# Boundaries between the blocks of a decoder step on one core: awaited stores, early loads, a later start of compression

## The chip, the cores and the metric

One core of a Trainium2 chip runs the whole step, one launch. The metric is the time of one launch in microseconds, the median of the runs shown.

## The reference

One layer of a decoder for two groups: a prompt of 1024 tokens, and 8 sample sequences with 4 new tokens each behind 8192 cached ones (all float32, model width 1024, heads of 64).

```
h = RMSNorm(x);  q, k, v, gates = h @ w_in
mixer A (8 heads): dilated windows (128,1), (512,4), (2048,16), merged by their denominators
mixer B (8 query heads, 2 key heads): compressed blocks of 64 tokens (an MLP over each),
  the 16 best blocks per token (gathered), and a window of 512; merged by sigmoid gates
every logit gets a bias from a table of relative positions
x += concat[A | B] @ w_out
h = RMSNorm(x);  u = h @ w_up;  causal depthwise convolution of width 3 (with kept state for samples)
x += (SiLU(gate) * value) @ w_down;  y = RMSNorm(x)
```
The caches, moved on by the new rows, are outputs too.

## The kernel before

The program is five blocks, each in a function of its own and run one after the other by `hybrid_step` (L3030). A block ends for each engine with its last instruction, a DRAIN, and a barrier of all engines (the lines of these are those on which a block is opened: L294, L1179, L1815, L865, L2372); then its semaphores are cleared (`Mem.end`, L65 to L69), with another barrier.

`front` (L150) projects all 1056 rows and compresses the sample caches. Its PE works through a list of jobs written out at L170 to L193: bias tables (b), transposes of x (x), projections by column chunk and row tile (n, s, f), transposes of keys (k), and queries and keys by chunk and group of rows (q). Compression is worked in 17 items of two halves. A half is one entry ("comp") in the order, 64 matmuls at L539 for the first item, over cache rows that POOL gathers and DVE turns (L721 for the first item, L730 for the others). L214 to L237 put the comps between the jobs: from job `first_c` on, one at most behind each job, spaced by the columns that the jobs multiply, and done 28000 columns ahead of the end. POOL issues the stores of results (L807 to L818) from five buffers and, last, waits for all of them and for the compressed rows of the prompt (L820 to L822).

`compressed_and_dilated` (cd, L1165) does the compressed branch for both groups and the dilated branch of the samples. SP issues its constants and queries (`qs`, `qp`, L1347 to L1359), then items of the dilated branch, the stores of the prompt's compressed output (L1373), the window keys for the block behind (L1377), and stores the dilated output to `mixT` in DRAM (L1382), which it waits for (L1384).

`sample_selected` (sb, L1804) does the selected and the window branch of the samples. SP loads the choice (L1942), the new keys (`knew`, L1944, L1945), window values, new values (L1947 to L1950), and at the end stores to `mixT` (L1953) and waits (L1955). ACT issues the window's bias `BW` in eight pieces (L2219) ahead of its copies. POOL gathers the chosen pages by indirect DMA (L116, L1974) and adds up their bias (L1984). PE starts with transposes of the new keys (L2011) and the window keys (L2017), later does the cached keys (L2080). DVE takes the window's scores with `BW` (L2259 to L2266).

`prompt_attention` (pa, L834) goes over 12 pairs of heads (3 kinds of 4), each in 8 query tiles. For a pair SP loads queries, keys, values and the bias of two heads (L920 to L936) into one of two buffers; POOL reverses the queries (L1036); PE multiplies (L969), transposes (L992) and multiplies by the values (L1012). At pair 9 SP loads `mixT` and, on 20 partitions, the state and weights of the convolution (`cv`, L953 to L955).

`ffn` (L2355) begins with the samples' part of the output projection (L2593), transposes `cv` (L2704), and then goes over all row tiles (L2611) and the up and down projections (L2652, L2730, L2680). Its SP starts with the rows of x (L2529) and an identity (L2530).

## Time and profile before

| | us |
|---|---|
| median of 3 runs | 2256.63 (2254.52 to 2258.96) |
| profiled execution | 2255.5 |
| its span, first to last instruction | 2253.5 |
| PE busy | 2108.8 (94%) |
| DVE / ACT / POOL busy | 1014.1 / 519.7 / 474.6 |
| mean granted clock of PE | 0.968 |

The span in 40 slices of 56 us, busy tenths of PE, its clock, and the DMA share:

```profile
PE   6989999997967885999999999999999999999998
...
PEclk9999999998788997999999999999999999999999
DMA  7467477643577996122251313665666332500200
```

A digit is the busy share of a slice in tenths. Front ends in the tenth slice, cd in the twelfth, sb in the sixteenth, pa in the twenty-second; the rest is ffn. "PEq", "SPq" are the sequencers of an engine: waits, branches and DMA issues.

### The profile page before, as it was taken

To read this page: it belongs to the slowest core of one execution; us is meant where nothing else is said; L and a number is where in the kernel's file an instruction comes from. 1 tells how busy PE (TensorE), PEld (TensorE's weight loads), DVE (VectorE), ACT (ScalarE), POOL (GpSimd) and SP (SyncE) were. 2 spreads that over 40 slices of the span, in tenths; PEclk is the share of its full clock that TensorE was granted. 3 is DMA by queue.
4 is the path that set the end of the run, shared out by engine and by line. 5 is a ranking of instruction groups with operands and counts; after the bars stand their busy time and mean duration, and the time that the engine had idled before them with its cause. 6 is when DMAs were issued, how large, how long until landed. Compare 5 with 4: busy or idle time off the path is not lost. (4 is left out here: it accounts for less than half of the span.)

```text
span 2253.5 us, 31733 instructions
## 1 busy us (share of the span) xinstructions
PE 2108.8 (94%) x12498; PEld 1374.5 (61%) x12498; DVE 1014.1 (45%) x2435; ACT 519.7 (23%) x1101; POOL 474.6 (21%) x667
## 2 busy tenths in 40 slices
PE   6989999997967885999999999999999999999998
PEld 3445466664635664666676446888888888544443
DVE  4044455402425543666676225667776765200110
ACT  3111101012213432776676111111111111000100
POOL 1434234102014650112222001223232222000000
PEclk9999999998788997999999999999999999999999
DMA  7467477643577996122251313665666332500200
GB/s 212 160 214 281 186 283 291 238 152 93 206 282 286 385 397 224 58 90 85 78 157 40 118 66 132 224 204 187 224 223 207 132 98 90 188 1 10 78 21 19
DMA packets 150649, 372.78 MB, mean 165 GB/s; under 512 B 36871, under 2 KB 89087, under 8 KB 132448
## 3 DMA queue, kind: packets, MB, share of 16 engines
q1 hardware_dynamic: 120678, 149.37, 21.0%
q0 software_dynamic: 25280, 149.44, 17.0%
q10 hardware_dynamic: 4544, 71.95, 9.0%
q8 instruction: 100, 1.64, 0.3%
q14 instruction: 47, 0.38, 0.1%
HBM read 343.42 MB, written 98.60 MB: 196 GB/s over the span
## 5 line engine op out<-in xcount | busy, mean ns | idle before, releaser
L2652 PE MATMUL ff_ps<-ff_hx,ff_aw 128*128 128x264 f32 x2464 | 550.1, 386 | 0.9 <-DVE ff_hx L2891 0.9
L2652 PEld LDWEIGHTS ff_ps<-ff_hx,ff_aw 128*128 128x128 f32 x2464 | 467.3, 190 | 80.8 <-issue 1.2
L730 DVE STREAM_TRANSPOSE sel_space<-sel_space 128x512 f32<-128x512 f32 x256 | 155.4, 674 | 165.6 <-PE in_psH L539 165.6
L503 PE MATMUL in_ps<-in_w,in_xT 128*128 128x512 f32 (+1 forms) x512 | 201.5, 547 | 0.0
L1113 DVE CUSTOM_DVE_ANT_0 pa_L<-pa_psS,pa_T 128x512 f32<-128x512 f32 (+3 forms) x288 | 138.9, 532 | 59.4 <-PE pa_psS L969 58.3
L1093 ACT ACTIVATE pa_L<-pa_L,pa_nm 128x640 f32<-128x640 f32 (+3 forms) x192 | 141.9, 741 | 45.1 <-DVE pa_nm L1123 43.2
L503 PEld LDWEIGHTS in_ps<-in_w,in_xT 128*128 128x128 f32 x512 | 95.0, 191 | 93.5 <-issue 87.6
L539 PE MATMUL in_psH<-sel_space 128*64 128x256 f32 (+1 forms) x1152 | 123.1, 369 | 11.2 <-DVE sel_space L721 11.2
L969 PE MATMUL pa_psS<-pa_kT,pa_qT 64*128 64x512 f32 (+3 forms) x576 | 114.9, 505 | 18.6 <-POOL pa_qT L1036 18.6
L628 ACT ACTIVATE in_yout<-in_ps 128x128 f32<-128x128 f32 (+5 forms) x88 | 41.3, 480 | 390.4 <-PE in_ps L503 213.4
L3013 DVE TENSOR_TENSOR ff_work<-ff_ps,ff_work 128x512 f32<-128x512 f32 (+1 forms) x18 | 12.3, 685 | 238.0 <-PE ff_ps L2730 139.3
L517 PE MATMUL in_ps<-in_xT,in_w 128*128 128x352 f32 x384 | 116.9, 462 | 0.0
L539 PEld LDWEIGHTS in_psH<-sel_space 128*64 128x64 f32 x1152 | 76.5, 142 | 59.6 <-issue 25.6
L992 PE MATMUL pa_psT<-pa_ident,pa_L 128*128 128x128 f32 x816 | 112.0, 281 | 0.4 <-DVE pa_PT L1139 0.2
L2611 PE MATMUL ff_ps<-ffn_G 128*128 128x512 f32 x256 | 111.9, 596 | 0.0
L992 PEld LDWEIGHTS pa_psT<-pa_ident,pa_L 128*128 128x128 f32 x816 | 87.2, 141 | 39.8 <-issue 18.6
L1012 PE MATMUL pa_psO<-pa_PT,pa_V 128*64 128x128 f32 x1632 | 110.3, 279 | 0.9 <-DVE pa_tmp L1151 0.5
L1087 ACT ACTIVATE pa_PT<-pa_psT 128x512 f32<-128x512 f32 (+2 forms) x182 | 91.9, 541 | 75.9 <-PE pa_psT L992 73.8
L2834 ACT ACTIVATE ff_work<-ff_work 128x1056 f32<-128x1056 f32 x22 | 23.8, 1084 | 368.3 <-DVE ff_work L2986 368.3
L2680 PE MATMUL ff_ps<-ff_hx,ffn_G 128*128 128x512 f32 x224 | 97.4, 592 | 0.0
L517 PEld LDWEIGHTS in_ps<-in_xT,in_w 128*128 128x128 f32 x384 | 72.0, 190 | 41.6 <-issue 3.5
L1012 PEld LDWEIGHTS pa_psO<-pa_PT,pa_V 128*64 128x64 f32 x1632 | 87.1, 136 | 16.5 <-issue 11.5
(381 smaller groups left out, 2671.0 us busy)
## 6 DMA issues: line engine op xcount, KB each, us to landing
out_new_a_k_s<-in_cache_a_k ACTq DMA_DIRECT2D x8, 4088.0 KB
out_new_a_v_s<-in_cache_a_v ACTq DMA_DIRECT2D x8, 4088.0 KB
ff_aw<-in_w_up SPq DMA_DIRECT2D x44, 512.0 KB, 7.8
in_w<-in_w_in SPq DMA_DIRECT2D x5, 2048.0 KB, 18.7
sel_space<-in_cache_a_k SPq DMA_DIRECT2D x8, 1024.0 KB
sel_space<-in_cache_a_v SPq DMA_DIRECT2D x8, 1024.0 KB
ff_hx<-in_w_down SPq DMA_DIRECT2D x14, 512.0 KB, 4.7
sel_space<-in_cache_a_k SPq DMA_DIRECT2D x24, 256.0 KB
```

The lines of the kernel that those rows point to most:

```text
L503: mm = pe.matmul(ps[0:n, b, 0:width], xT[:, k, t * P:t * P + n], w[:, at % WBUF, k, 0:width], start=(k == 0), stop=(k == KC - 1))
L517: mm = pe.matmul(ps[:, b, 0:n], w[:, at % WBUF, k, c * P:c * P + P], xT[:, k, r0:r0 + n], start=(k == 0), stop=(k == KC - 1))
L539: mm = pe.matmul(psH[dh * HD:dh * HD + HD, r % 2, o0:o0 + n], w1[:, kv, t16, dh, :], rows[:, dh, t, :], start=(t16 == 0), stop=(t16 == 15) ...
L730: last = dve.transpose(put[:, dh, :, k * HD:k * HD + HD].rearrange("p t (g b) -> p t g b", g=2), got[:, :, :, dh, :])
L969: pe.matmul(psS[:, c % 2, h, 0:w], qT[r, i, qt * P:qt * P + P], kT[r, i, j0 * P + k0:j0 * P + k0 + w], start=True, stop=True).then_inc(s_q ...
L992: mm = pe.transpose(psT[:, b % 3, (x - x0) * P:(x - x0) * P + P], turned, ident[:, :])
L1012: mm = pe.matmul(psO[h * HD:h * HD + HD, u % 2, 0:P], V[:, i, j0 + j, v0:v0 + HD], PT[:, u % 3, (2 * j + h) * P:(2 * j + h) * P + P], star ...
L1093: nc.scalar.activation(x, x, ACT.Exp, bias=nm[:, s, h:h + 1], scale=1.0, accum_out=sm[:, s, h:h + 1]).then_inc(s_ex, 1)
L1113: dve.tensor_tensor_reduce(L[:, u % 3, h, 512 * x:512 * x + n], psS[:, c % 2, h, 0:n], T[:, it % 2, h, SEQ - w + 512 * x:SEQ - w + 512 * x ...
L2611: mm = pe.matmul(ps[:, j % 6, :], mixT[:, k, t * P:t * P + P], wo[:, k, half * 512:half * 512 + 512], start=(k == 0), stop=(k == KC - 1))
L2652: mm = pe.matmul(ps[:, bank_of(x, j, g), 0:H2], aw[:, j % 2, at, k, :], hx[:, bt, k, g * H2:g * H2 + H2], start=(k == 0), stop=(k == KH - 1))
L2680: mm = pe.matmul(ps[:, bank[i] + half, :], G[:, k, t * P:t * P + P], wd(k)[:, half * 512:half * 512 + 512], start=(k == 0), stop=(k == NFF ...
```

## The change

- In front the jobs from which comps are placed begin four later (`first_c`).
- The semaphores of front's stores outlive the block. Its POOL waits only for the prompt's compressed rows; the other stores are awaited by SP in cd, ahead of `qs` and `qp`, which move behind `tails`, `rows` and `graws`.
- cd doesn't wait for its store to `mixT`; it issues the two loads of the new keys for sb, ahead of the window keys.
- A class `Operands` gives the operands of pa's pairs places that are free in sb already, in the area that holds the gathered pages and, later, the activations of ffn. sb's SP issues queries, keys and values of the first pair once the last cached keys are transposed, and its bias once all but the last scores are there. sb doesn't wait for its stores to `mixT`; pa's SP waits for the three `mixT` stores at pair 9. pa issues only pair 1 and on at its start.
- The identity of the first blocks is kept for pa and ffn, which no longer load one.
- The three loads of `cv` move from pair 9 of pa to the start of ffn, ahead of x.
- To make room, the large area is allocated once for the whole program, ffn's work area lies at its end, some small tiles of cd share one area, and `yout` is allocated last in front.

```diff
+class Operands:
+
+    NKIND = 3
+    QT = SEQ // P
...
+        first = KC * (ROWS + D)
+        slot = [first, first + 3 * SEQ]
+        self.qL = [at(o, SEQ) for o in slot]
+        self.kT = [at(o + SEQ, SEQ) for o in slot]
+        self.V = [at(o + 2 * SEQ, SEQ).rearrange("p (t n) -> p t n", n=P) for o in slot]
+        self.T = [at(6 * Selected.SLOT + i * 2 * SEQ, 2 * SEQ).rearrange("p (h n) -> p h n", h=2) for i in range(2)]
+        self.mix = at(slot[1] + 3 * SEQ, 4 * NB * NT).rearrange("p (r b t) -> p r b t", r=4, b=NB)
+        self.s_ld = [m.sem(f"pair_loaded{i}") for i in range(2)]
+        self.s_mixed = m.sem("sample_mix_stored")
...
+    def load_rows(self, sp, it):
+        kd, p, i = self.kinds[it // 4], it % 4, it % 2
+        q0 = (kd["q0"] + 2 * p) * HD
+        sp.dma_start(self.qL[i], self.scr["qT"][q0:q0 + P, 0:SEQ]).then_inc(self.s_ld[i], 16)
+        vsrc = (self.scr if kd["v"] in self.scr else self.io)[kd["v"]].rearrange("(t p) n -> p t n", p=P)
+        if it // 4 == 0:
+            k0 = 2 * p * HD
+            sp.dma_start(self.kT[i], self.scr["kT"][k0:k0 + P, 0:SEQ]).then_inc(self.s_ld[i], 32)
+            sp.dma_start(self.V[i], vsrc[:, :, p * P:p * P + P]).then_inc(self.s_ld[i], 16)
...
+    def load_bias(self, sp, it):
+        kd, p, i = self.kinds[it // 4], it % 4, it % 2
+        tab = self.scr[kd["tab"]]
+        width = tab.shape[1]
+        back = min(self.QT, kd["back"] + 1) * P
+        for h in range(2):
+            src = bass.AP(tab.tensor, (kd["q0"] + 2 * p + h) * width + kd["tab0"] + SEQ - back, [[1, P], [1, back]])
+            sp.dma_start(self.T[i][:, h, SEQ - back:SEQ], src).then_inc(self.s_ld[i], 16)
...
-    first_c = last_prompt + 5
+    first_c = last_prompt + 9
...
-            for b in range(NP):
-                pool.wait_ge(s_st[b], total[b])
             pool.wait_ge(s_ps, 32)
+
+    return total
...
-            load(0)
-            sp.dma_start(ident[:, :], io["c_ident"][:, :]).then_inc(s_id, 16)
+                ops.load_rows(sp, it)
+                ops.load_bias(sp, it)
+
             load(1)
...
                 if it == 9:
+                    sp.wait_ge(ops.s_mixed, 48)
                     sp.dma_start(mixT[:, :, SEQ:ROWS], scr["mixT"].rearrange("(k p) n -> p k n", p=P)).then_inc(s_mix, 16)
-                    sp.dma_start(cv[0:2 * NB, :], io["state_conv"][:, :]).then_inc(s_cvl, 16)
-                    sp.dma_start(cv[2 * NB:2 * NB + 3, :], io["conv_w"][:, :]).then_inc(s_cvl, 16)
-                    sp.dma_start(cv[2 * NB + 3:2 * NB + 4, :], io["conv_b"][:, :]).then_inc(s_cvl, 16)
...
-            for g in range(2):
-                sp.dma_start(qs[g * HD:g * HD + HD, :, :],
-                             scr["qT"][512 + g * 256:768 + g * 256, SEQ:ROWS].rearrange("(r d) n -> d r n", d=HD)).then_inc(s_c, 16)
-            sp.dma_start(qp[:, :, :], scr["qT"][512:1024, 0:SEQ].rearrange("(c p) n -> p c n", p=P)).then_inc(s_c, 16)
...
+            for sem, n in stores:
+                sp.wait_ge(sem, n)
+            for g in range(2):
+                sp.dma_start(qs[g * HD:g * HD + HD, :, :],
+                             scr["qT"][512 + g * 256:768 + g * 256, SEQ:ROWS].rearrange("(r d) n -> d r n", d=HD)).then_inc(s_c, 16)
+            sp.dma_start(qp[:, :, :], scr["qT"][512:1024, 0:SEQ].rearrange("(c p) n -> p c n", p=P)).then_inc(s_c, 16)
...
             sp.wait_ge(s_out, 16)
+            sp.dma_start(knew[:, 0, :], scr["s_w"][:, 0:P]).then_inc(s_nl, 16)
+            sp.dma_start(knew[:, 1, :], io["new_slc_k_s"][:, :]).then_inc(s_nl, 16)
             sp.wait_ge(d_tr, use["keys", NB - 1, NTL - 1] + 1)
...
             sp.wait_ge(d_cd, copied(use["out", 1])[1])
             sp.dma_start(scr["mixT"][0:512, 0:RS].rearrange("(c p) n -> p c n", p=P),
-                         mixA[:, :, :, :].rearrange("p c b t -> p c (b t)")).then_inc(d_st, 16)
-            sp.wait_ge(d_st, 16)
+                         mixA[:, :, :, :].rearrange("p c b t -> p c (b t)")).then_inc(s_mixed, 16)
...
-            sp.dma_start(knew[:, 0, :], scr["s_w"][:, 0:P]).then_inc(s_nl, 16)
-            sp.dma_start(knew[:, 1, :], io["new_slc_k_s"][:, :]).then_inc(s_nl, 16)
...
+            sp.wait_ge(s_tr, use["keys", NB - 1, 1, 3] + 1)
+            ops.load_rows(sp, 0)
+            sp.wait_ge(s_qk, NB * NQ - 1)
+            ops.load_bias(sp, 0)
             sp.wait_ge(s_f, 10)
             for g in range(2):
                 sp.dma_start(scr["mixT"][512 + g * 256:768 + g * 256, :].rearrange("(r d) n -> d r n", d=HD),
-                             mix[g * HD:g * HD + HD, :, :, :].rearrange("p r b t -> p r (b t)")).then_inc(s_st, 16)
-            sp.wait_ge(s_st, 32)
+                             mix[g * HD:g * HD + HD, :, :, :].rearrange("p r b t -> p r (b t)")).then_inc(ops.s_mixed, 16)
 
...
+            sp.dma_start(cv[0:2 * NB, :], io["state_conv"][:, :]).then_inc(s_cvl, 16)
+            sp.dma_start(cv[2 * NB:2 * NB + 3, :], io["conv_w"][:, :]).then_inc(s_cvl, 16)
+            sp.dma_start(cv[2 * NB + 3:2 * NB + 4, :], io["conv_b"][:, :]).then_inc(s_cvl, 16)
             for i in range(3):
                 t = order[i]
                 sp.dma_start(xin[i][0:rows_of(t), :], x_rows(t)).then_inc(s_x[i], 16)
-            sp.dma_start(ident[:, :], io["c_ident"][:, :]).then_inc(s_id, 16)
             sp.dma_start(gain1, io["norm_ffn"].partition_broadcast(P)).then_inc(s_gn, 16)
...
             out_parts()
             pe.wait_ge(s_cvl, 48)
-            pe.wait_ge(s_id, 16)
```

## Rows read from the trace of the kernel before

**Rows 1.** The page: shares of the span by engine, along the chain that ended last
```profile
PE 44%; DVE 0%; DMA 0%; ACT 0%; SPq 0%; issue 0%
```

**Rows 2.** The chain of waits, pieces in time: start us, us, what
```profile
1237.63 0.33 SPq L2529
...
1244.27 4.85 PE ff_ps L2704 x44
```

**Rows 3.** What PE waited for: us in total, times, longest
```profile
PE pa_psS L969 <- POOL pa_qT L1036: 18.6, 1, 18.6
...
PE sb_psT L2011 <- DMA sb_knew<-out_new_slc_k_s: 11.9, 1, 11.9
...
PE ff_ps L2704 <- DMA ff_ident<-in_c_ident: 2.8, 1, 2.8
```

**Rows 4.** Timeline of PE, 104 to 141: start us, us, engine line, instructions
```profile
108.05 7.03 PE L503 MATMUL in_ps<-in_w,in_xT 128*128 128x512 f32 x16
...
127.24 3.68 PE L539 MATMUL in_psH<-sel_space 128*64 128x64 f32 x64 [11.18 <-DVE sel_space L721]
...
138.00 2.09 PE L539 MATMUL in_psH<-sel_space 128*64 128x64 f32 x64
```

**Rows 5.** Line L721 (ns min/median/max, first and last start); L730 (busy, idle)
```profile
L721 DVE STREAM_TRANSPOSE sel_space<-sel_space x4: 1201/1202/1246, 124.7 to 128.1; 128x1024 f32<-128x1024 f32 x4
...
L730 DVE STREAM_TRANSPOSE sel_space<-sel_space 128x512 f32<-128x512 f32 x256 | 155.4, 674 | 165.6 <-PE in_psH L539 165.6
```

**Rows 6.** Timelines of POOL and PE around the end of front
```profile
520.83 0.54 POOL L818 DMA_DIRECT2D scr_qT<-in_yout  x1 [4.19 <-ACT in_yout L628]
...
529.53 2.89 PE L1408 MATMUL cd_psT<-sample_ident,sel_space 128*128 128x128 f32 x12 [9.50 <-PEq L69]
```

**Rows 7.** Line L294, front's exit: duration ns, first and last start us
```profile
L294 POOLq COMPARE_BRANCH  x1: 33/33/33, 523.2 to 523.2; - x1
L294 POOLq DRAIN  x1: 5132/5132/5132, 523.4 to 523.4; - x1
```

**Rows 8.** Timeline of SP, 655 to 684, the end of cd
```profile
657.64 2.29 SPq L1377 DMA_DIRECT2D sel_space<-in_cache_win_k  x2
669.76 0.38 SPq L1382 DMA_DIRECT2D scr_mixT<-cd_mixA  x1
```

**Rows 9.** Timelines of ACT, DVE and PE in the first 26 us of sb
```profile
672.64 4.74 ACTq L2219 DMA_DIRECT2D sb_BW<-scr_tabW  x8
...
693.89 1.81 DVE L2264 TENSOR_TENSOR sb_mtw<-sb_mxw 128x1 f32<-128x1 f32 x1
...
698.39 1.12 PE L2080 MATMUL sb_psT<-sample_ident,sel_space 128*128 128x128 f32 x4 [4.49 <-ACT sel_space L2224]
```

**Rows 10.** Transfers in 690 to 692.4, by queue: packets, MB, share of 16 engines
```profile
q10 hardware_dynamic: 20, 0.03, 4.0%
```

**Rows 11.** Timeline of SP, 870 to 892, from sb to pa
```profile
875.40 1.32 SPq L1953 DMA_DIRECT2D scr_mixT<-sb_mix  x2
879.64 0.36 SPq L920 DMA_DIRECT2D pa_qL<-scr_qT  x1
```

**Rows 12.** Line L1815, sb's exit, and line L1036, pa's reversal of the queries
```profile
L1815 SPq COMPARE_BRANCH  x1: 33/33/33, 878.1 to 878.1; - x1
...
L1036 POOL COPY pa_qT<-pa_qL x12: 1036/1041/1045, 890.9 to 1201.4; 128x1024 f32<-128x1024 f32 x12
```

**Rows 13.** Windows at the end of sb: us, busy by engine, PE clock, DMA share, GB/s
```profile
845.00:850.00 5.00, 4.56 (x40) 3.16 (x36) 3.38 (x7) 2.41 (x5) 0.00 (x0) 1.00 1.00 415
...
855.00:860.00 5.00, 3.74 (x101) 2.44 (x90) 1.01 (x4) 0.35 (x2) 1.14 (x2) 1.00 0.01 3
```

**Rows 14.** Timeline of SP, 1165 to 1182, pa's pair 9
```profile
1168.43 4.40 SPq L953 DMA_DIRECT2D ffn_G<-in_state_conv  x1
...
1173.22 0.24 SPq L955 DMA_DIRECT2D ffn_G<-in_conv_b  x1
```

**Rows 15.** Transfers in 1176 to 1180.5, SP's queue: packets, MB, share
```profile
q1 hardware_dynamic: 11, 0.07, 8.1%
```

More of the change, by code:

```diff
@@ L152, in front @@
+def front(nc, io, scr, pre, idx, ident, kcs, vcs, s_st, s_ps):
     NP = 5
@@ L355, in front @@
         s_ev = [m.sem("job_out_by_act"), m.sem("job_out_by_dve")]
-        s_st = [m.sem(f"stored{i}") for i in range(NP)]
         s_w1 = m.sem("compression_weights_loaded")
@@ L831, in backwards, with prompt_attention @@
     return bass.AP(x.tensor, x.offset + step * (cols - 1), [[part, n], [step * cols, tiles], [-step, cols]])
-def prompt_attention(nc, io, scr, mixT, wo, cv, s_mix, s_wo, s_cvl):
+def prompt_attention(nc, io, scr, mixT, wo, ident, ops, s_mix, s_wo):
     QT = SEQ // P
-    NKIND = 3
+    NKIND = ops.NKIND
     NIT = NKIND * 4
     U = NIT * QT
-    kinds = [
-        dict(tab="tabA", tab0=7172 - A0, q0=0, k0=0, v="new_a_v_p", gate=None, back=QT),
-        dict(tab="tabS", tab0=7172, q0=8, k0=8, v="new_slc_v_p", gate=1, back=QT),
-        dict(tab="tabW", tab0=7172 - W0, q0=8, k0=10, v="vw", gate=2, back=LW // P),
-    ]
+    kinds = ops.kinds
+    qL, kT, V, T, s_ld = ops.qL, ops.kT, ops.V, ops.T, ops.s_ld
     def parts(u):
@@ L892, in prompt_attention @@
         s_gs = m.sem("gates_ready")
-        s_ld = [m.sem(f"pair_loaded{i}") for i in range(2)]
         s_qr = m.sem("queries_reversed")
@@ L1161, in _, with compressed_and_dilated @@
                     finish(s - 3)
-def compressed_and_dilated(nc, io, scr, mixB, GB, Qb, pre, ident, kcs, vcs):
+def compressed_and_dilated(nc, io, scr, mixB, GB, Qb, pre, ident, kcs, vcs, knew, s_nl, s_mixed, stores):
     QT = SEQ // P
@@ L1194, in compressed_and_dilated @@
         PTs = Ps
-        score = [m.sb(f"score{i}", [NR, NBLK + 1]) for i in range(3)]
+        score = [early[0:NR, 4 * NBLK:5 * NBLK + 1]] + [m.sb(f"score{i}", [NR, NBLK + 1]) for i in (1, 2)]
         top8 = m.sb("top8", [NR, 2, 8])
         pen = m.sb("pen", [NR, NBLK])
-        graw = m.sb("graw", [1, 2, RS * 24 // 2])
         qp = m.sb("qp", [P, 4, SEQ])
@@ L2352, in _, with ffn @@
                 dve.tensor_tensor(mix[h, :, :, :], *halves, ALU.add).then_inc(s_f, 1)
-def ffn(nc, io, scr, G, mixT, wo, cv, s_mix, s_wo, s_cvl, s_moved):
+def ffn(nc, io, scr, G, spare, mixT, wo, cv, ident, s_mix, s_wo, s_moved):
     NCV = 2 * NB + 4
@@ L3032, in hybrid_step @@
     s_moved = kernel_stack.enter_context(nc.semaphore("windows_moved"))
+    whole = Mem(nc, kernel_stack, "whole")
+    space = whole.sb("space", [P, 7 * Selected.SLOT])
+    ident = whole.sb("ident", [P, P])
+    ops = Operands(whole, io, scr, space)
+    s_st = [whole.sem(f"stored{i}") for i in range(5)]
+    s_ps = whole.sem("prompt_compressed_stored")
+    s_nl = whole.sem("new_keys_loaded")
+    s_mix = whole.sem("sample_mix_loaded")
+    s_wo = whole.sem("output_weights_loaded")
     with ExitStack() as stack:
```

113 lines of the change are left out of this document (42 added, 71 removed).

## The prediction

> **What bounds the kernel now.** I read the page first. Matmul (PE) is busy 94% of the span of 2253.5 us, and the chain that ended last, 44% of the span, is PE in every piece that counts [rows 1]. The chain of waits reaches back only to the start of ffn: there SP's first load is issued at 1237.63, and the convolution transposes start at 1244.27; what comes behind them is matmuls back to back [rows 2]. So ffn costs what it costs, and this change can act only where PE stands idle: in front, at the four boundaries between blocks, and through the clock that it finds after an idle time. The second view is therefore what PE waited for [rows 3]: 18.6 us for POOL's reversal at the start of prompt_attention (pa), 11.9 us for the new keys at the start of sample_selected (sb), 2.8 us in ffn for an identity. Beside these stand 11.18 us ahead of the first compression [rows 4] and 9.50 us between front and compressed_and_dilated (cd) [rows 6]. PE idle at the five places: 54 us. Any end that is moved moves everything behind it one for one, as PE has no slack to hide it in. The edits are costed in their order in time; the profiled run took 2255.5 us, and each gain is taken off that.
>
> **Compression four jobs later.** The first half item's 64 matmuls waited 11.18 us for the DVE transpose, and ran in 3.68 us; the next half's same 64 took 2.09 us [rows 4], so they ran at the lower clock. The transposes are four of 1.2 us starting at 124.7 [rows 5], done at about 129.3; the first batch was usable at 127.24. The change puts four jobs in front: two of sixteen 128x512 matmuls (7.03 us each in [rows 4]) and two short ones. PE works from 116.05 to at least 130.1 on them, later than 129.3: the idle time is gone, and with it the low clock. The work is the same, only its order changes. Gain 11.18 + (3.68 - 2.09) = 12.8 us. Cost: the 34 half items now share 0.93 of the columns they had; DVE's 256 transposes waited 165.6 us for PE and were 155.4 us busy [rows 5], so they have room for that. I put this at 0; the ends are -2 (gathers that come late once or twice) and +1.
>
> **POOL doesn't wait for its last stores.** The last store is issued at 520.83 [rows 6]; POOL leaves its waits at 523.2. But it then stands in a DRAIN of 5.132 us until 528.5 [rows 7], and the barrier follows; cd's matmuls start at 529.53 [rows 6]. Without the wait the DRAIN begins at 521.4. If it lasts 5.1 us whenever it begins, the gain is 523.2 - 521.4 = 1.8 us. If it lasts until the stores are over, it is 0; if it is short when nothing was waited for, up to 7.3 us. I take 1.8: the stores had signalled before this DRAIN began, and it still took 5.1, so it wasn't their data that it stood for. cd's SP now waits for those stores before it loads qs and qp; these stand last but for the dilated items, and the first item loads there wait for DVE anyhow. That wait is over at the latest by 523.2, before cd's SP starts: 0.
> The trace has the store over 2.4 us after its issue (520.83 to 523.2). The Trainium skill, "DMA: Bandwidth & Descriptors", section on the anatomy of one DMA, gives about 2 us plus bytes by 436 GB/s for such a store, mostly the receipt of the write, which by itself would make the boundary worth the 2 us and leave nothing for a DRAIN: the trace agrees with the 2.4 us and shows 5.1 us more that the page doesn't have.
>
> **cd's mixT store and the new keys.** The store is issued at 669.76, 0.38 us long [rows 8], and sb's first issues come at 672.64 [rows 9]; the barrier itself costs 1.0 us (528.5 to 529.53 above). Without the wait sb starts at 671.2, 1.4 us earlier. PE needs the new keys and the window keys: both are issued in cd now, the new ones beside the window keys that went out at 657.64 [rows 8]; there is time to 667. So PE would start at 671.3 and not at 681.11, 9.8 us earlier. But it won't keep that. ACT issues the window bias in eight pieces from 672.64 on, and packets of its queue still run at 692.4 [rows 10], none in the 7.5 us after. DVE's window softmax stands on it, then stalls 1.81 us in a TENSOR_TENSOR on a single column, ACT does its exps, and only then copies for PE, which waits 4.49 us until 698.39 [rows 9]. This chain starts with the bias, and the bias moves only by the 1.4 us of the block, by some 0.35 us for the two loads less ahead of it, and 1.65 us for the stall, of which I leave the next operations' 0.16 us, as POOL's large operation no longer meets it. So 1.4 + 0.35 + 1.65 = 3.4 us. The ends are 1.4, where the stall stays, and 12.4, the 9.8 and the 2.5 us more that the warm clock and the earlier gathers give, where the bias is in time.
> The two vnew loads, now earlier on SP's queue by the two that went, land ahead of their use: 0.
>
> **The first prompt pair, and sb's mixT stores.** The last store is issued at 875.40 + 1.32 = 876.72 [rows 11]; SP's wait lasts until 878.1 [rows 12], and pa's first load goes out at 879.64, 1.5 us after it [rows 11, 12]. POOL's reversal waits for all of the pair's loads until 890.9 [rows 12]. With the pair loaded ahead, the block starts at 876.72 + 1.5 = 878.2, and POOL reverses at once: 890.9 - 878.2 = 12.6 us. Price: 2.5 MB come in the last 30 us of sb, beside value gathers; in 845:850 the DMA engines run at share 1.00 and 415 GB/s [rows 13]. They are idle from 855 to 860, so most of the gathers' delay is made up. I take 0.3, and at most 2.5 MB / 0.415 MB per us = 6.1 us. Gain 12.3. The store to mixT is awaited by SP at pair 9, some 290 us on, next to the first row of [rows 14]: 0. Flip and gates come one load earlier: 0.
>
> **Identity and convolution loads in ffn.** The 2.8 us for the identity end [rows 3]. But the three convolution loads are issued here now, ahead of x. In before, SP took 4.40 us to issue the first, at a time when the queue was full, and the last was issued at 1173.22 [rows 14]. In the window 1176 to 1180.5 the queue still took 8.1% of 16 engines, 5.8 us of one engine, for three packets of 22 KB [rows 15]: rows on one partition, about 1.9 us each, and the last one over at 1180 at the latest. That is 6.8 us from the last issue. In ffn the issues start at 1237.63 [rows 2]; with an empty queue the third goes out at 1238.9, landing at 1245.7 against 1244.27 before: -1.4 us. Ends: +2.8 and 1.8 of clock if the rows are as fast as ordinary ones, -5.0 if the first issue takes 4.40 us here too.
>
> **Sum.** 12.8 + 1.8 + 3.4 + 12.3 - 1.4 = 28.9 us. 2255.5 - 28.9 = 2226.6 for the profiled run; it lies 1.1 us below the median, so the median goes to 2227.7.
>
> **The rivals.**
> *The bias is no gate.* PE meets sb's window work 9.8 us earlier, the gathers start earlier with it, and the bias lands sooner since ACT's queue has less beside it. Against it stand the 4.49 us of PE behind that chain. It gives 9.0 us more: 2218.7.
> *The pair's loads hold up the gathers.* The values of the last sequences then come late by up to 6.1 us, in place of 0.3: 2233.5. For it: share 1.00 at 845:850; against it: the idle 5 us that follow. The Trainium skill, same page, section on queues, rings and completion order, has each engine take turns between queues packet by packet, so a gather beside the pair's loads would get about half the rate; by that rule this rival is the more likely one. The trace shows the share of both, not who got which.
> *The change doesn't do what it says at two boundaries.* The DRAIN ends with the stores (0 in place of 1.8) and the convolution rows land at the late end (-5.0): 5.4 us less, 2233.1.
> *Slower.* Compression begins four jobs later and must end at the same place, so PE meets a gather or transpose that isn't ready at every item. 17 items; it decides from 28.9 / 17 = 1.7 us per item, and is slower by 0.2% from (28.9 + 4.5) / 17 = 2.0 us each: 2261 and more. Against it: 165.6 us of DVE waiting for PE [rows 5], and a 7% shift in spacing.
>
> **How the numbers follow.** A measurement of this kernel can tell 0.2%, 4.5 us, from no change. Chances: forecast 0.62, bias no gate 0.14, gathers held up 0.10, two boundaries fail 0.09, slower rival 0.05, of which 0.02 beyond +0.2% and 0.02 within. The forecast's own bounds, taking the nearer ends of each part, reach from -6 to +6; with the rivals at 2218.7 and 2233.5 and some 3 us for the phase of PE's clock the range is 2215 to 2238. Faster 0.96, same 0.02, slower 0.02.
>
> **What would show it.** No wait of PE ahead of the first compression and its 64 matmuls at 2.1 us; a POOL DRAIN of 5 us still behind front's last store; PE starting sb within 0.3 us of the barrier, and then a wait of some 11 us (4.49 + 9.8 - 3.4) behind ACT's copies; PE starting pa within 2.5 us of the block; a wait for the convolution rows of 4 us in ffn. The forecast is wrong if PE waits for compression transposes at many items, if cd's first waits grow by what front lost, or if the last values of sb come late.

## The result and the profile after

The changed kernel takes 2239.32 us, median of 5 runs (2238.28 to 2244.34), against 2254.52 for the kernel before, median of 5: ratio 0.9933, interval 0.9918 to 0.9948, so 15.2 us faster. A second session gave 2238.36 against 2257.4 (0.9914, 0.9896 to 0.9931). The forecast was 28.9 us less and a median of 2227.7, worked out from a median of 2256.63 before; the upper end of its range was 2238. The profiled run took 2238.28 us, its span 2235.9.

The page's slices of the changed kernel (busy tenths of PE, clock, DMA share):

```profile
PE   6999999998967987999998999999999999999998
...
PEclk9999999998878998999999999999999999999999
DMA  8477577635686985232252214656665432400200
```

PE's third slice (first compression) rose from 8 to 9, the tenth (front to cd) from 7 to 8 and the sixteenth (sb to pa) from 5 to 7; the twelfth, where sb begins, stays at 6. What PE waited for (us in total, times, longest), the rows that answer to [rows 3] and those that are new:

```profile
PE sb_psT L2089 <- ACT whole_space L2233: 17.9, 8, 9.0
...
PE pa_psS L979 <- POOL pa_qT L1044: 6.2, 1, 6.2
PE cd_psT L1419 <- PEq L69: 5.4, 1, 5.4
PE ff_ps L2713 <- DMA whole_space<-in_conv_b: 4.5, 1, 4.5
...
PE sb_psV L2078 <- DMA sb_vnew<-out_new_slc_v_s: 3.0, 1, 3.0
...
PE sb_psT L2020 <- PEq L69: 2.4, 1, 2.4
```

The reversal's 18.6 us are 6.2, the keys' 11.9 are 2.4 of barrier, front's 9.50 are 5.4, and no wait ahead of compression is left. In their place stand 9.0 us behind ACT's copies at one point of sb (4.49 in [rows 9]; 17.9 is the sum of eight), 3.0 for the new values, and 4.5 for the convolution rows (2.8 for the identity).

To see where the 28.9 us went, the span is cut at the first and last matmul of each block in PE's timeline. Profiles of one kernel differ in some stretches, so the table takes all whose PE work in that stretch is the same (in cd and in the two gaps, all with the same code there):

| stretch of PE | before (2 profiles) | with the change | forecast | measured |
|---|---|---|---|---|
| front, first to last matmul | 511.1, 511.1 | 498.6 (mean of 15) | -12.8 | -12.5 |
| front to cd, idle | 9.50, 9.50 | 5.43 | -1.8 | -4.1 |
| cd | 139.6, 139.7 | 139.6 (mean of 10) | 0 | 0.0 |
| cd's last to sb's last matmul | 204.3, 209.4 | 213.2, 213.0, 212.2, 210.2, 209.5, 207.7 (mean 211.0) | -3.1 | +4.1 |
| sb to pa, idle | 18.56, 18.66 | 6.25 | -12.6 | -12.4 |
| ffn | 1007.8, 1005.2 | 1011.9 (mean of 13) | +1.4 | +5.3 |

The last column sums to -19.6, beside -15.2 and -19.0 of the medians. Three rows came as forecast, one was better, and sb (7.2 us) and ffn (3.9 us) were worse. The spread within a row matters: cd took 136.7 to 142.3 us over all profiles with the change, and the two profiles of before differ by 5.1 us in sb and 2.6 in ffn.

### The profile page after: what moved, and what is told of

It is laid out like the page before. It is cut to its first block and busy times, and to the rows that moved or that the text cites. A ratio compares the mean times of both kernels' runs of the same rounds, so it can differ in the third digit from the quotient of the medians.

```text
span 2235.9 us, 31725 instructions
## 1 busy us (share of the span) xinstructions
PE 2113.8 (95%) x12498; PEld 1374.8 (61%) x12498; DVE 1019.4 (46%) x2435; ACT 518.9 (23%) x1101; POOL 472.4 (21%) x667
## 5 line engine op out<-in xcount | busy, mean ns | idle before, releaser
L776 DVE STREAM_TRANSPOSE whole_space<-whole_space 128x512 f32<-128x512 f32 x256 | 155.3, 675 | 153.5 <-PE in_psH L585 153.5
L1121 DVE CUSTOM_DVE_ANT_0 pa_L<-pa_psS,whole_space 128x512 f32<-128x512 f32 (+3 forms) x288 | 138.9, 532 | 47.2 <-PE pa_psS L979 45.8
L585 PE MATMUL in_psH<-whole_space 128*64 128x256 f32 (+1 forms) x1152 | 121.6, 364 | 0.0
L2992 DVE SCALAR_TENSOR_TENSOR whole_space<-whole_space,ff_kept 128x1024 f32<-128x1024 f32 x88 | 120.2, 1366 | 3.1
L979 PE MATMUL pa_psS<-whole_space,pa_qT 64*128 64x512 f32 (+3 forms) x576 | 115.0, 505 | 6.2 <-POOL pa_qT L1044 6.2
L3021 DVE TENSOR_TENSOR whole_space<-ff_ps,whole_space 128x512 f32<-128x512 f32 (+1 forms) x18 | 12.3, 685 | 238.0 <-PE ff_ps L2739 139.3
L1000 PE MATMUL pa_psT<-whole_ident,pa_L 128*128 128x128 f32 x816 | 112.0, 281 | 0.4 <-DVE pa_PT L1147 0.2
L2621 PE MATMUL ff_ps<-whole_space 128*128 128x512 f32 x256 | 112.3, 597 | 0.0
L1000 PEld LDWEIGHTS pa_psT<-whole_ident,pa_L 128*128 128x128 f32 x816 | 87.2, 141 | 39.8 <-issue 17.6
L1020 PE MATMUL pa_psO<-pa_PT,whole_space 128*64 128x128 f32 x1632 | 110.3, 279 | 0.9 <-DVE pa_tmp L1159 0.5
L2690 PE MATMUL ff_ps<-ff_hx,whole_space 128*128 128x512 f32 x224 | 97.4, 592 | 0.0
## 6 DMA issues: line engine op xcount, KB each, us to landing
in_w<-in_w_in SPq DMA_DIRECT2D x5, 2048.0 KB, 12.5
```

What stands on the lines that cost most here:

```text
L585: mm = pe.matmul(psH[dh * HD:dh * HD + HD, r % 2, o0:o0 + n], w1[:, kv, t16, dh, :], rows[:, dh, t, :], start=(t16 == 0), stop=(t16 == 15) ...
L776: last = dve.transpose(put[:, dh, :, k * HD:k * HD + HD].rearrange("p t (g b) -> p t g b", g=2), got[:, :, :, dh, :])
L1000: mm = pe.transpose(psT[:, b % 3, (x - x0) * P:(x - x0) * P + P], turned, ident[:, :])
L1121: dve.tensor_tensor_reduce(L[:, u % 3, h, 512 * x:512 * x + n], psS[:, c % 2, h, 0:n], T[it % 2][:, h, SEQ - w + 512 * x:SEQ - w + 512 * x ...
L2621: mm = pe.matmul(ps[:, j % 6, :], mixT[:, k, t * P:t * P + P], wo[:, k, half * 512:half * 512 + 512], start=(k == 0), stop=(k == KC - 1))
L2690: mm = pe.matmul(ps[:, bank[i] + half, :], G[:, k, t * P:t * P + P], wd(k)[:, half * 512:half * 512 + 512], start=(k == 0), stop=(k == NFF ...
```

## The experiments

Every one but the first starts from the changed kernel, three_ahead from the kernel three. A stretch is always the one from cd's last to sb's last matmul, the gap the one between front and cd.

**How far one profile can be trusted.** The kernel before, a second time.

> The kernel before, profiled a second time. From the last matmul of compressed_and_dilated to the last of sample_selected it took 204.3 us; five profiles of the changed kernel and its variants gave 207.7 to 214.6 for the same stretch, with one to three short spells of the lower clock in the part where the DMA engines are full, against one in before. Theory 1 (the stretch of before is 204 us and its spells of low clock are few): again 203 to 206. Theory 2 (the spells come by chance in either kernel): 206 to 211.

2256.49 us, ratio to before 0.9988 (0.9966 to 1.0009). The stretch from cd to sb's end took 209.4 us, and not 204.3: theory 2. In the records of the clock it has 37.5 us at the lower level against 30.7, among them two spells of 3.4 us in the part in which the DMA engines are full, where the first profile had one. The changed kernel has such spells too; here the 5 us before one, the spell itself and the time just behind it (columns as in [rows 13]):

```profile
760.50:765.50 5.00, 3.05 (x26) 1.80 (x24) 2.73 (x7) 2.83 (x4) 3.78 (x5) 1.00 0.99 387
765.50:768.90 3.40, 3.00 (x13) 1.01 (x14) 0.77 (x2) 0.83 (x2) 2.78 (x4) 0.53 1.02 426
770.00:773.40 3.40, 3.40 (x31) 2.29 (x30) 2.49 (x5) 1.42 (x3) 3.25 (x2) 1.00 1.02 426
```

Two numbers of the stretch go with its length: PE's idle time and its time at the low clock, of which half counts. Before, they were 36.5 and 30.7 us, and 38.4 and 37.5 in the second profile; in the changed kernel 39.4 and 39.4, in a second profile of it 38.0 and 41.9. With the idle time and half of the low time taken off, 152 to 154 us are left in these four profiles, and 152 to 159 in all. The idle time is no shorter than before although its first 9.5 us are gone.

**The part on the new keys undone.**

```diff
-            sp.dma_start(knew[:, 0, :], ...)       # in cd, both loads
+            sp.wait_ge(s_mixed, 16)                # at cd's end
+            sp.dma_start(knew[:, 0, :], ...)       # at sb's start, both loads
```

> The changed kernel with one part undone: the new keys are loaded at the start of sample_selected again, and the block ahead waits for its store. In the changed kernel that block took 18.5 us longer than before from its first matmul to its last, although it began 9.5 us sooner behind the block ahead. Theory 1 (what is loaded inside the block sets its pace: the window bias, then the new values): PE waits some 12 us for the keys again, and the wait behind ACT's copies (9.0 us in the changed kernel) falls to 4 to 5; the time rises by 1 to 4 us, to 2240 to 2243. Theory 2 (the early start was worth its 9.5 us and something else ate the rest): it rises by 9 us or more, 2248 and up. Theory 3 (the early start itself brought the losses further on in the block): it falls, 2236 or less.

2242.8 us (2235.52 to 2245.23; the profiled run is the fastest of them), stretch 208.7 us, wait for the keys 11.8 us and behind ACT's copies 4.5 at most. The time and the waits are those of theory 1, but the stretch is shorter than with early keys, as by theory 3. So it was repeated beside the changed kernel:

> The changed kernel again, beside the next three on one chip. From the last matmul of compressed_and_dilated to the last of sample_selected six profiles with this code took 207.7 to 214.6 us, mean 211.2. Both theories: 207 to 215 here, and a time about 15 us below before.

> keys_late again, beside after_again. Theory 1 (PE's early start gives nothing: what it saves at the start comes back as waits for loads of the block): within 2.5 us of after_again. Theory 2 (it gives what its end of the gate gave in the forecast, 3.4 us, hidden so far by chance): 3 to 5 us slower than after_again. Theory 3 (it costs: more spells of low clock behind the new waits): 2.5 us or more faster.

2238.36 us for the changed kernel and 2241.38 with the keys late, ratios 0.9914 (0.9896 to 0.9931) and 0.9924 (0.9901 to 0.9947); stretches 213.0 and 214.5. The changed kernel's 19.0 us below before are more than the 15 expected. The 3.0 us between the two lie inside the intervals. Early keys are worth 0 to 3 us, and don't cost anything; theory 3 falls, theories 1 and 2 aren't told apart.

**Window bias and new values loaded in cd.**

```diff
-                    act.dma_start(BW[g * NT + t:P:8, :], ...)      # sb, eight
-            sp.dma_start(vnew[:, 0, :, :], ...)                     # sb, two
+            # the same ten loads by SP in cd, behind those of knew
```

> The changed kernel with the window bias and the new values loaded in the block ahead too, behind the new keys (in the place of operands that are dead by then). Theory 1 (these loads set the pace of the first 40 us of sample_selected): the 9.0 us wait behind ACT's copies and the 3.0 us wait for the new values both go, and about 3 us of low clock with them: 10 to 15 us off the changed kernel's 2239, 2224 to 2229. Theory 2 (the stage is bound by the gathers that follow, whatever comes early): the waits go and others for gathers come in their place, 0 to 4 us off, 2235 to 2239.

2237.61 us, ratio 0.9921 (0.9905 to 0.9938), the changed kernel's within the interval; stretch 211.3. The time is theory 2's. Waits of PE in sb:

```profile
PE sb_psT L2097 <- ACT whole_space L2235: 13.3, 8, 4.5
...
PE sb_psT L2028 <- DMA whole_space<-in_cache_win_k: 7.1, 1, 7.1
...
PE sb_psV L2086 <- DMA whole_space<-in_cache_win_v: 5.0, 1, 5.0
```

The 9.0 us fell to 4.5, but 7.1 us for the window keys (behind ten more loads on SP's queue) and 5.0 for the window values came in their place; theory 2 had waits for gathers there. So the bias that the forecast took for the one gate isn't the only one: three sets of loads come in within a few us of each other.

**The first value gathers behind.**

```diff
-            for c in range(NQ):
-                values(0, c)
             bias(0)
             for b in range(1, NB + 1):
                 for c in range(NQ):
                     if b < NB:
                         keys(b, c)
+                    if b == 1 and c == 1:
+                        for x in range(NQ):
+                            values(0, x)
```

> The changed kernel with POOL's four value gathers of the first sequence put behind the first two key gathers of the second, so that they no longer run beside the loads at the start of sample_selected (window bias, window values, new values). Theory 1 (the block's own loads and these gathers share full DMA engines for the first 27 us, and PE's window values wait for the last of them, whatever PE does earlier): the waits of 9.0 and 3.0 us shrink by 5 us or more together, the key gathers that PE needs next come no later, and the time falls by 4 to 8 us, to 2231 to 2235. Theory 2 (the gathers only move: the engines are full later on as well, so the same bytes come out of the same time): the early waits shrink but the end stays, 2237 to 2241.

> values_behind again, beside after_again. If the value gathers beside the block's own loads are what holds PE, 6 to 9 us faster than after_again; if its first result came from few spells of low clock, 0 to 4.

2230.76 us (0.9861, 0.9833 to 0.989), just theory 1's, and in the second session 2226.32 (0.9866, 0.9844 to 0.9888) beside the changed kernel's 2238.36: 12 us, more than the 6 to 9 expected. The stretch took 204.0 and 198.7 us. First the start of sb in the changed kernel (PE's timeline: start us, us, instructions, idle before), and what the DMA engines did in two pieces of it, then the same instructions in values_behind2:

```profile
653.62 0.39 PE L2020 MATMUL sb_psT<-whole_ident,sample_knew 32*128 32x32 f32 x2 [2.40 <-PEq L69]
...
665.68 3.47 PE L2089 MATMUL sb_psT<-whole_ident,whole_space 128*128 128x128 f32 x28
678.20 1.11 PE L2089 MATMUL sb_psT<-whole_ident,whole_space 128*128 128x128 f32 x4 [9.04 <-ACT whole_space L2233]
...
689.54 1.08 PE L2078 MATMUL sb_psV<-whole_space,sb_PTw 128*32 128x128 f32 x32 [2.96 <-DMA sb_vnew<-out_new_slc_v_s]
```

```profile
660.00:665.00 5.00, 5.00 (x52) 3.91 (x54) 2.29 (x5) 1.19 (x2) 4.33 (x2) 0.67 1.04 371
...
670.00:675.00 5.00, 0.00 (x0) 0.00 (x0) 0.47 (x1) 0.00 (x0) 1.87 (x2) 0.85 1.01 367
```

```profile
655.84 0.39 PE L2021 MATMUL sb_psT<-whole_ident,sample_knew 32*128 32x32 f32 x2 [2.40 <-PEq L69]
...
674.05 0.65 PE L2090 MATMUL sb_psT<-whole_ident,whole_space 128*128 128x128 f32 x4 [2.88 <-ACT whole_space L2234]
...
681.60 1.06 PE L2079 MATMUL sb_psV<-whole_space,sb_PTw 128*32 128x128 f32 x32
```

In the changed kernel PE is through with what it has at 669.15 and stands until 678.20; the engines carry 366 to 371 GB/s at full share in 660:675. It reaches the window values (L2078) at 689.54, 35.9 us after its first matmul in sb. In values_behind2 the same points come 18.2 us (24.6 in the changed kernel) and 25.8 us after the first matmul. In the first profile, values_behind, they come at 24.3 and 32.7 us, so only part of this shows there; in three, below, at 18.2 and 25.8 again.

SP's timeline shows what PE waits for there. SP loads the window values and then the new values in two loads; the first lines are before, then the changed kernel, then values_behind2:

```profile
683.17 11.12 SPq L1949 DMA_DIRECT2D sb_vnew<-scr_s_w  x1
694.34 0.71 SPq L1950 DMA_DIRECT2D sb_vnew<-out_new_slc_v_s  x1
```

```profile
661.25 14.69 SPq L1955 DMA_DIRECT2D sb_vnew<-scr_s_w  x1
675.99 0.79 SPq L1956 DMA_DIRECT2D sb_vnew<-out_new_slc_v_s  x1
```

```profile
661.45 4.95 SPq L1955 DMA_DIRECT2D sb_vnew<-scr_s_w  x1
666.45 0.33 SPq L1956 DMA_DIRECT2D sb_vnew<-out_new_slc_v_s  x1
```

In the changed kernel SP stands 14.69 us in the issue of the first, and the second goes out 24.8 us after cd's last matmul, hardly sooner than before (25.2). With the gathers behind it goes out after 13.0 us. In the first 25 us after cd's last matmul POOL's queue carries 5.4 MB in the changed kernel and 3.8 in values_behind2, SP's queue 1.9 and 2.7. The early stage of sb is bound by the bytes ahead of PE's operands, and the gathers are a part that nobody needs yet. The Trainium skill, "DMA: Bandwidth & Descriptors", section on queues, rings and completion order, says that an engine takes turns between its queues packet by packet; this fits, as gathers on POOL's queue slowed loads on SP's and ACT's.

**The same with the keys late.**

> The changed kernel with the first value gathers behind (as in values_behind) and the new keys late again (as in keys_late). values_behind took 204.0 us from the last matmul of compressed_and_dilated to the last of sample_selected; keys_late 208.7, the changed kernel and four variants with the same code there 207.7 to 214.6. Theory 1 (idle time that early keys remove is real once the loads of the block no longer gate it): the stretch is 3 to 8 us longer than in values_behind, 207 to 212, and the time 2234 to 2239. Theory 2 (the early keys are worth nothing in either case, since what PE does there isn't what the stretch waits for): 202 to 206, time 2229 to 2233.

> keys_late_vb again, beside values_behind2. Theory 1 (the early start is worth nothing even with the gathers out of the way, as the bias and window values still come later than PE): within 2.5 us of values_behind2. Theory 2 (it is worth something once they are out of the way): 3 to 8 us slower than values_behind2.

2230.56 us (0.9895, 0.9875 to 0.9914), and 2229.47 (0.9878, 0.9858 to 0.9899) beside 2226.32; stretches 205.5 and 199.7. Late keys cost 3.1 us here in medians, inside the intervals, and 1.0 to 1.5 in the stretch. The wait for them and the one behind ACT's copies in the second profile:

```profile
PE sb_psT L2091 <- ACT whole_space L2235: 11.7, 8, 2.9
PE sb_psT L2022 <- DMA sample_knew<-out_new_slc_k_s: 9.3, 1, 9.3
```

So 9.3 us of wait are worth some 1 to 3 us, with the gathers gone as well. That is theory 2 of the first expectation; of the second, the medians are just theory 2's, and the stretch would be theory 1's.

**The first prompt pair loaded late.**

```diff
-            ops.load_rows(sp, 0)      # sb
-            ops.load_bias(sp, 0)      # sb
+            load(0)                   # pa, ahead of load(1)
             load(1)
```

> The changed kernel with the first prompt pair loaded at the start of prompt_attention, as before. Theory 1 (the early load costs the block ahead nothing): PE's wait at the start of prompt_attention grows from 6.2 to 18 us, sample_selected keeps its length of some 211 us, and the time rises by 12 us to 2251. Theory 2 (the early load delays the last gathers by up to 6.1 us, which would explain part of the block's 18.5 us): sample_selected gets 4 to 6 us shorter and the time rises by 6 to 8 us only, 2245 to 2247.

2249.32 us, ratio 0.9966 (0.9952 to 0.9981), 10 us above the changed kernel (7 to 12 by the ratios), between the 12 of theory 1 and the 6 to 8 of theory 2; PE's wait at pa's start:

```profile
PE pa_psS L980 <- POOL pa_qT L1045: 17.1, 1, 17.1
```

The stretch of sb took 214.6 us without the early loads, the longest of all, and not 4 to 6 us shorter. Theory 1: these loads cost the gathers nothing that can be seen. They fill what was free. First the changed kernel with the pair's bias on its way, then the 5 us at nearly the same distance from the start of sb (192 us, against 191) without it (columns as in [rows 13]):

```profile
845.00:850.00 5.00, 4.94 (x114) 2.97 (x106) 0.11 (x3) 0.28 (x1) 0.94 (x1) 1.00 1.05 381
```

```profile
848.00:853.00 5.00, 4.69 (x134) 3.38 (x126) 0.88 (x3) 0.28 (x1) 0.50 (x1) 1.00 0.07 25
```

**Front's end.** POOL waits again:

```diff
+            for b in range(NP):
+                pool.wait_ge(s_st[b], total[b])
             pool.wait_ge(s_ps, 32)
```

> The changed kernel with POOL waiting for all of its stores at front's end again. Theory 1 (the wait and the DRAIN add up, and a DRAIN that begins behind signalled stores still takes 5.1 us): a gap of 9.5 us between front and the next block again, 4.1 more than the changed kernel. Theory 2 (my forecast: the DRAIN takes the same time whenever it begins): the DRAIN takes 3.5 us as in the changed kernel, and the gap is 7.2 us, 1.8 more.

2236.56 us (2 runs), gap 7.27 us, 1.84 above the changed kernel's 5.43. Theory 2, the forecast's: the wait is worth 1.8 us, as read from the gap; the median of two runs doesn't show it. But the DRAIN behind it (duration in ns, start) is 2.93 us here and 5.13 in [rows 7]:

```profile
L342 POOLq DRAIN  x1: 2927/2927/2927, 510.1 to 510.1; - x1
```

In the changed kernel:

```profile
L342 POOLq DRAIN  x1: 3472/3472/3472, 507.9 to 507.9; - x1
```

What shortened it is another part of the change. Compression begun at the former place:

```diff
-    first_c = last_prompt + 9
+    first_c = last_prompt + 5
```

> The changed kernel with compression begun at the former place in front. By my forecast: PE waits 11.2 us again ahead of the first 64 matmuls, which take 3.7 us, and the time rises by 12.8 us, to 2252. For the gap behind front, 5.4 us in the changed kernel: theory 1 (the later compression, not the dropped wait, made POOL's DRAIN shorter than in before): 7.2 to 7.8 us again, with a DRAIN of 5 us; theory 2 (it has nothing to do with it): 5.4 us.

2252.76 us, 13.4 above the changed kernel, where 12.8 were expected; front took 11.8 us longer and the gap 2.1. The DRAIN, and PE's wait in front:

```profile
L342 POOLq DRAIN  x1: 5537/5537/5537, 520.4 to 520.4; - x1
```

```profile
PE in_psH L585 <- DVE whole_space L767: 11.2, 1, 11.2
```

5.5 us of DRAIN and a gap of 7.49: theory 1. Why four jobs of other work in front change what POOL stands for 400 us later isn't settled by these runs; POOL's own list of gathers and stores is the same but for their order. Last, the final eight stores issued by SP:

```diff
+            for j in span_of[5][4:]:
+                wait_out(sp, j)
+                sp.dma_start(scr["qT"][...], yout[:, j % NP, 0:rows]).then_inc(s_st[lane(j)], 16)
```

> The changed kernel with the last eight stores of queries in front issued by SP, idle by then, and not by POOL; 5.4 us of PE lie between front and the next block in the changed kernel, 9.5 in before. Theory 1 (POOL's DRAIN at the block's end stands until its own last DMAs are through, 3.5 us here): the DRAIN is short, the gap is 1.5 to 2.5 us, and the time falls by 3 to 4 us. Theory 2 (the DRAIN takes 3.5 to 5 us whenever POOL issued anything in the block, or the barrier waits for something else): the gap stays at 5.4 and the time at 2239.

2233.85 us (0.9879, 0.9852 to 0.9906), gap 4.15. Between the theories: POOL's last DMA lies 38 us back, and its DRAIN still takes 2.3 us. The gap is 1.3 us shorter than in the changed kernel, which doesn't account for the whole difference of the medians. cd took 137.9, 136.7 and 136.8 us in the three profiles with these stores (the other two are three and three_ahead) and 138.8 to 142.3 in the others; no run tells whether that is the stores' doing.

```profile
L345 POOLq DRAIN  x1: 2273/2273/2273, 509.8 to 509.8; - x1
```

**Convolution rows transposed behind the second out tile.**

```diff
-            (44 transposes of cv)
             out_sum()
             for i in range(1, NTILE + 2):
                 if i < NTILE:
                     out_tile(i)
+                if i == 1:
+                    (44 transposes of cv; DVE's copies at i == 2)
```

> The changed kernel with PE's transposes of the convolution's rows moved behind the second out tile in ffn, and DVE's copies of them with them; nothing ahead of ffn is touched. Theory 1 (PE waited 4.5 us for rows that are slow to load, and ran at the lower clock behind that wait): the wait goes, ffn gets 4.5 to 7 us shorter, 2232 to 2235. Theory 2 (the rows are late by more than the tiles cover, or DVE's later copies hold up the first transposes): under 2 us. As nothing ahead of ffn differs, it also tells whether the 210.8 us of sample_selected, of which 5.4 us come late in the block without a new wait of over 3 us, stand: by theory 1a they do (209 to 212), by theory 1b they were a chance of that execution (203 to 207).

Two of its four runs took 2224.95 and 2224.67 us; two others 3625 and 5475, of which I know no cause; the kernel three below, with the same edit, had nothing like it in five runs. So its profile is used and not its median. SP's issues and PE's timeline in the changed kernel:

```profile
1216.53 0.34 SPq L2535 DMA_DIRECT2D whole_space<-in_state_conv  x1
...
1217.27 0.24 SPq L2537 DMA_DIRECT2D whole_space<-in_conv_b  x1
```

```profile
1216.73 5.07 PE L2603 MATMUL ff_ps<-whole_space 128*32 128x512 f32 x32 [1.89 <-PEq L69]
1226.35 4.79 PE L2713 MATMUL ff_ps<-whole_ident,whole_space 20*128 20x20 f32 x44 [4.54 <-DMA whole_space<-in_conv_b]
```

The third load goes out 0.7 us after the first (forecast: 1.3), and PE gets the rows 9.1 us after it, not 6.8. PE in cv_later:

```profile
1220.18 14.00 PE L2621 MATMUL ff_ps<-whole_space 128*128 128x512 f32 x32
1234.11 2.91 PE L2718 MATMUL ff_ps<-whole_ident,whole_space 20*128 20x20 f32 x44
```

And the first 45 us of ffn in the changed kernel and in cv_later:

```profile
1216.50:1261.50 45.00, 40.23 (x140) 18.52 (x141) 8.84 (x14) 5.18 (x9) 5.01 (x4) 0.85 0.51 137
```

```profile
1215.00:1260.00 45.00, 45.00 (x172) 20.50 (x165) 11.40 (x20) 6.70 (x13) 5.89 (x4) 1.00 0.58 160
```

ffn takes 999.9 us in place of 1011.9, where my theory said 4.5 to 7 us less. PE is busy 45.0 of 45 us and the clock stays at its upper level. Of the 12 us not all belong to the edit: three and three_ahead, below, have it too and take 1002.8 and 1002.9 us, 9 less. They have a spell of 10.2 us at the lower clock 127 us into ffn, far from any wait; cv_later has none there, and the 13 profiles without the edit have one of 3.4 to 10.2 us. In these 13 PE is idle for 9.7 us of ffn and at the lower clock for 18.9 (means); in the three with the edit 4.1 to 4.9 and 0 to 10.2. So the idle time behind the first 32 matmuls cost its own length and the half speed of what followed, some 10 us together. The same profile's sb stretch, 207.7 us with unchanged code, lies between theories 1a and 1b and is the lower end of those with this code; 213 is the upper.

**All three together, and with the early bias.**

> The changed kernel with three edits that each made it faster alone: first value gathers behind (7 us less in the stretch of sample_selected against the mean of the others), convolution transposes behind the second out tile (11.7 us less in ffn), SP issuing front's last eight stores (1.3 us less). They touch different blocks, so if each removes idle time or low clock of its own they add up: 20 us less than the changed kernel's 2239, 2219. If part of their gain was the chance of a few spells of low clock, 2221 to 2227.

> The kernel three with the window bias and the new values loaded in the block ahead, behind the window keys this time (ahead of them they made the window keys 7.1 us late in ahead_both). Theory 1 (with the value gathers behind, the bias is what PE still waits for behind ACT's copies): the wait of some 9 us there falls to under 3, and the time falls by 5 us or more against three, to 2214 or less. Theory 2 (the window values and gathers gate the stretch anyway): PE waits for the window values instead, and the time is that of three within 2 us.

three: 2211.05 us, median of 5 (2209.13 to 2217.36), ratio to before 0.9804 (0.9786 to 0.9823). That is 28 us below the changed kernel, 8 more than the sum expected; the stretch is 197.6 us (211.0 the mean without the edit), ffn 1002.8, the gap 4.15, cd 136.7.

```profile
PE sb_psT L2101 <- ACT whole_space L2245: 11.7, 8, 2.9
```

three_ahead: 2214.59 us (0.9816, 0.9795 to 0.9837), not faster: its stretch is 200.8. Theory 1 falls, as the wait behind ACT's copies was 2.9 us in three already. Theory 2 has the direction, but not its wait for window values, and the time is 3.5 us above that of three, with intervals that overlap.

## Why the prediction was wrong

**Compression four jobs later** was right, 12.5 of 12.8 us. The changed kernel's timeline shows the first of the jobs in front and the 64 matmuls at full speed:

```profile
115.30 7.13 PE L549 MATMUL in_ps<-in_w,in_xT 128*128 128x512 f32 x16
...
130.11 2.08 PE L585 MATMUL in_psH<-whole_space 128*64 128x64 f32 x64
```

**POOL's wait** was right as a mechanism, 1.84 us (pool_waits) of 1.8. But the step "if it lasts 5.1 us whenever it begins" took the DRAIN for a constant, and it became shorter by 2.1 us by another part of the change (5.54 us in comp_early, 3.47 in the changed kernel). The gain was 4.1; that it came out above the forecast is luck.

**The new keys and what waits behind them** failed. The step "this chain starts with the bias, and the bias moves only by ..." named one gate where there were three: bias, new values, window values. The step "the two vnew loads ... land ahead of their use: 0" missed the next one. The bias's gate kept its place nearly as said (a wait of 9.0 us at L2089, where 11 were forecast), and PE left it 27.0 us after cd's last matmul, 2.2 sooner than before (29.2) and 0.8 sooner than in before_again (27.8). But its first matmul on the window values came 38.2 to 38.4 us after cd's last in all seven profiles with this start of sb, and 37.6 and 37.9 us after it in the two of before: 0.5 us later, where the forecast has 3.4 sooner. It waited 3.0 to 3.9 us there for the new values; in before it didn't wait there, in before_again for 2.6. As SP's lines above show, the second of these loads went out no sooner than before.

One thing that can keep the engines full came with the early keys. POOL's next key gathers wait for PE's transposes of the window keys. First before, then the changed kernel:

```profile
688.88 0.97 POOL L116 DMA_INDIRECT sel_space<-in_cache_slc_k,sample_idx  x1 [6.15 <-PE sb_psT L2017]
```

```profile
664.10 0.96 POOL L116 DMA_INDIRECT whole_space<-in_cache_slc_k,sample_idx  x1 [0.67 <-issue]
```

That is 19.7 and 12.9 us after cd's last matmul. So gathers went beside the block's own loads some 6 us sooner; no run moves these gathers alone, so what they cost isn't shown. Late keys put the window values at 39.5 and 39.8 us, so early ones are worth some 1.3 us up to there. With the first gathers behind it is 32.2 and 31.7 with late keys, and with early ones 28.2 in values_behind2 and in three, but 35.1 in values_behind.

The clock isn't the reason up to this point: PE's low-clock time to it is 20.5 to 22.3 us, and was 23.9 and 17.1. The other 3.6 us of the row lie behind it, where PE's code is the same: 166.7 and 171.5 us before, 169.4 to 174.9 in the six profiles of the table. This isn't explained. From 5 to 20 us after the block's start the engines carry 357 to 373 GB/s in the profiles with unchanged gathers, and 379 and 392 in the two of before, at the same full share, which is some 5% of 15 us, 1 us; the rest stays open, and with two profiles of before it could be chance. Sb is longer than before with the keys late too (208.7 and 214.5 against 204.3 and 209.4), and early keys don't cost anything (they are worth 0 to 3 us, keys_late2).

The rival that the bias is no gate pointed to the wrong side: it held that without this gate PE would be quicker, and ahead_both showed the next gate directly behind it.

**The first pair** was right, 12.35 of 12.3 us with its price; the rival of gathers held up fell with pair_late. The rule on turns between queues in the Trainium skill, "DMA: Bandwidth & Descriptors", section on queues, rings and completion order, had made that rival the likelier one. It fits the start of sb, where the engines are full and PE waits; at the block's end the idle spell of [rows 13] took the loads up (a DMA share of 1.05 in 845:850 of the changed kernel, of 0.07 without the loads).

**ffn** failed in size: +1.4 was +5.3. The transposes of `cv` begin 9.4 us after the block's first matmul in the mean of 13 profiles, and 6.5 us after it before: 2.9 us later, where 1.4 were forecast. The term that was too small is the landing, 6.8 us behind the last issue, which was 8.6 to 9.2 here. It had been taken from a stretch with an idle queue behind the rows; here rows of x, the gain and weights came right behind them on the same engines, whose share is 0.86 in the block's first 5.4 us and 0.99 in the wait. That this is the reason is argued, not tested.

The other 2.4 us go with the clock, for which the sum had no term; only its better end had one, 1.8 us. PE's time at the lower clock in ffn is 18.9 us in the mean of the 13, and 13.7 and 10.2 in the two profiles of before. It isn't the spell behind the wait alone that grew: in the two kernels' profiled runs that one is as long (the first line is before, the second the changed kernel; the clock is the third number from the end):

```profile
1244.30:1252.70 8.40, 8.40 (x49) 5.34 (x49) 2.05 (x4) 0.00 (x0) 1.26 (x1) 0.50 1.06 279
```

```profile
1226.35:1234.70 8.35, 8.35 (x49) 5.29 (x49) 1.82 (x3) 0.00 (x0) 0.81 (x1) 0.51 0.94 266
```

Over the first 60 us the low-clock time is 11.6 us (mean of 13) against 10.2 and 6.8, and beyond them 7.4 against 3.4 and 3.4, in a spell that begins 133 to 140 us into ffn and whose cause no run shows.

**The sum.** Each gain was taken as if an idle us removed were a us gained, but for the bias. At the first compression and at the start of pa that held. Where the block behind is bound by its own loads it is wrong, and where the idle time grows it can cost more than its length. Three small slips change nothing: 9.8 and 2.5 are 12.3, not 12.4; the DRAIN's upper case is 528.5 - 521.4 = 7.1, not 7.3; and 890.9 - 878.2 is 12.7.

## What to carry to other kernels

A wait at the start of a block is worth what it hides only if nothing else in the block is timed from the block's start: list every load issued there, and ask which of them PE meets in the next 40 us. If the DMA engines are full in that time, take bytes away that nobody needs yet before loading operands sooner. And ask what an engine that starts sooner sets going: here POOL's gathers. Put PE work that is ready between the issue of a small slow load and its use: here some 5 us of idle time saved came with as much again from the clock.

## What the runs showed of the hardware

POOL's DRAIN at the end of front took 5.1 us in before, 5.5 in comp_early, 3.5 in the changed kernel, 2.9 behind signalled stores and 2.3 with no DMA of its own in the last 38 us; so it isn't only the wait for its last stores, and it is longer with an order of work that differs only far ahead of it. SP stood 11.1 and 13.8 us in the issue of one small load in the two profiles of before, 14.7 in the changed kernel and 4.9 in values_behind2, with the engines full. Two profiles of one kernel differed by 5 us in a stretch of 205, 3.4 of them by time at the lower clock; PE had been busy 3.05 of the 5 us before the spell shown above. Moving 44 transposes saved 9 to 12 us of ffn, of which some 5 were idle time.
